# Feed-forward parts of a two-block network on one core: most chunks with the weights as stationary operand, without transposes

## The reference

```
def _rmsnorm(x, g):
    xf = x.astype(jnp.float32)
    y = xf * lax.rsqrt(jnp.mean(xf * xf, axis=-1, keepdims=True) + EPS)
    return (y * g.astype(jnp.float32)).astype(x.dtype)

def _swiglu(x, wg, wu, wd):
    return (jax.nn.silu(x @ wg) * (x @ wu)) @ wd

h = _swiglu(_rmsnorm(x, g[0]), ffn_w_gate[l, 0], ffn_w_up[l, 0], ffn_w_down[l, 0])
x = x + 0.5 * _rmsnorm(h, g[1])
```

## Time and profile before

| | |
|---|---|
| median of 3 runs | 1312.46 us (1311.19 to 1315.73) |
| span of the profiled execution | 1310.4 us, first to last instruction |
| its own time | not given apart from the span |
| TensorE busy, matmuls | 1287.3 us, 98% |
| VectorE busy | 783.8 us, 60% |
| ScalarE busy | 680.9 us, 52% |
| GpSimd busy | 118.8 us, 9% |
| granted TensorE clock, mean | 0.997 |
| memory traffic | 253.64 MB, mean 194 GB/s |

### The profile page before, as it was taken

The page is one execution under the profiler, slowest core; times in us unless marked ns, Lnnn a source line. Parts: engine busy times, 40 slices in busy tenths (PEclk is TensorE's granted clock), DMA queues, the critical chain, the costliest instruction groups (busy, mean ns, idle before and its releaser), DMA issues.

```text
span 1310.4 us, 18569 instructions
## 1 busy us (share of the span) xinstructions
PE 1287.3 (98%) x6815; PEld 1059.7 (81%) x6815; DVE 783.8 (60%) x1029; ACT 680.9 (52%) x1025; POOL 118.8 (9%) x120
## 2 busy tenths in 40 slices
PE   8999999999999999999999999999999999999997
PEld 7887788887788887877888888888887897888886
DVE  4477655454855556576655556655556677755554
ACT  4433643344744455557644447544556656745543
...
GB/s 336 380 402 211 140 295 203 180 187 177 161 193 192 192 203 182 194 178 91 195 194 180 183 200 146 207 192 192 185 231 98 185 152 102 189 191 183 181 206 54
DMA packets 177379, 253.64 MB, mean 194 GB/s; under 512 B 9352, under 2 KB 143796, under 8 KB 177332
## 3 DMA queue, kind: packets, MB, share of 16 engines
...
## 4 chain that ended last, share of the span: by engine, by line
PE 91%; DVE 4%; ACT 2%; SPq 1%; DMA 1%; issue 1%; DVEq 0%; ACTq 0%
PE ps L601 27%; PE ps L603 26%; PE ps L602 26%; PE ps L641 2%; PE ps L686 2%; PE ps L642 2%; PE ps L649 2%; PE ps L1011 1%; PE ps L625 1%; PE ps L883 1%; DMA raw<-in_conv_w_in 1%; SPq L480 1%; ACT L1177 1%; PE ps L872 1%; DVE x_sb L1714 1%
## 5 line engine op out<-in xcount | busy, mean ns | idle before, releaser
L1658 DVE TENSOR_TENSOR w_lo<-raw,w_hi 128x2048 fp32r<-128x2048 f32 x111 | 261.8, 2359 | 158.9 <-ACT w_hi L1189 158.8
L601 PE MATMUL ps<-w_lo,xT_hi 128*128 128x512 f32 x836 | 331.2, 396 | 1.0 <-DVE act_pair L1815 1.0
L603 PE MATMUL ps<-w_hi,xT_lo 128*128 128x512 f32 x836 | 326.2, 390 | 0.0
L602 PE MATMUL ps<-w_hi,xT_hi 128*128 128x512 f32 x836 | 325.7, 390 | 0.0
L1663 DVE SCALAR_TENSOR_TENSOR w_lo<-raw,par,w_hi 128x512 fp32r<-128x512 f32 x336 | 231.6, 751 | 133.2 <-ACT w_hi L1194 133.1
L1189 ACT ACTIVATE w_hi<-raw 128x2048 fp32r<-128x2048 f32 x111 | 212.2, 1913 | 152.3 <-PE ps L603 144.1
L1194 ACT ACTIVATE w_hi<-raw,par 128x512 fp32r<-128x512 f32 x336 | 214.4, 712 | 0.8 <-PE ps L603 0.8
L603 PEld LDWEIGHTS ps<-w_hi,xT_lo 128*128 128x128 f32 x836 | 156.9, 188 | 33.5
L601 PEld LDWEIGHTS ps<-w_lo,xT_hi 128*128 128x128 f32 x836 | 157.0, 188 | 33.3 <-DVE act_pair L1815 1.4
L602 PEld LDWEIGHTS ps<-w_hi,xT_hi 128*128 128x128 f32 x836 | 157.2, 188 | 31.4 <-issue 0.2
L601 PE MATMUL ps<-w_lo,hT_hi 128*128 128x512 f32 x400 | 156.5, 391 | 0.0
(11 more groups left out here) (256 smaller groups left out, 1497.1 us busy)
## 6 DMA issues: line engine op xcount, KB each, us to landing
...
```

The source lines that it names most:

```text
L601: pe.matmul(o, a_hi, b_lo, start=first, stop=False, skip_group_check=True)
L602: pe.matmul(o, a_hi, b_hi, start=False, stop=False, skip_group_check=True)
L603: return pe.matmul(o, a_lo, b_hi, start=False, stop=last, skip_group_check=True)
L1658: dve.tensor_tensor(w_lo[:, slot_of(n), :], raw[:, slot_of(n), :], w_hi[:, slot_of(n), :].bitcast(F32), ALU.subtract).then_inc(raw_done, 1)
```

## The change

In chunks 1 to 10 of every feed-forward part the first product is done the other way round. `wide_part` takes 128 columns of weights as stationary operand and all 256 tokens as moving one. For each of four column blocks (two of gates to banks 2 and 3, two of up to banks 0 and 1) and each input tile there are two matmuls: the low weights against `xT_hi`, 256 columns, and the high weights against `xT_hi` and `xT_lo` together, 512 columns, into the two halves of a bank. For the latter the two tensors become one, `xT_pair`. The sums come out with hidden columns on the partitions, which is what `down_part` needs, so these chunks have no transposes. Chunk 0 stays as it was, except that its turned form goes through bank 4.

The two halves of a bank have to be added. ScalarE copies the second half (`gate_rest`, `up_rest`) and VectorE adds the first. Tokens now lie along the columns, so r is needed as a row on every partition: `turn_r` makes it once a part with two transposes, ScalarE copies it to `r_cols`, and VectorE multiplies the gates by it. The up half isn't multiplied by r any more; as the result is normalised behind the part, the epsilon of that norm is scaled instead (`EPS_Y`).

TensorE's order in a chunk j is `next_wide(j)` (first unit), `wide_up(j)` (second unit), and `down(j)` for chunk j - 1. At the end of a part, `down` of chunk 9 is done for the first token tile and half of the second before the wait for the last chunk, and one group of six matmuls instead of twelve stays behind `y_tok0`. The table load on ScalarE stands between the last silu and the last up copy. In FFN0 the gate rows are summed between the groups of `down`, and ScalarE copies both behind `yT_hi`.

```diff
+        xT_pair = sb("xT_pair", [P, 2, KT, SEQ], F32R)
+        xT_hi, xT_lo = xT_pair[:, 0, :, :], xT_pair[:, 1, :, :]
         yT_hi = sb("yT_hi", [P, KT, SEQ], F32R)
         yT_lo = sb("yT_lo", [P, KT, SEQ], F32R)
...
-            def turn_hid(s, j):
+            def turn_hid(bank):
                 for f in range(2):
                     for t in range(TOKT):
-                        tr = pe.transpose(ps[:, 2, f * SEQ + t * P:f * SEQ + (t + 1) * P], hid[:, t, tok(f)], ident[:, :])
+                        tr = pe.transpose(ps[:, bank, f * SEQ + t * P:f * SEQ + (t + 1) * P], hid[:, t, tok(f)], ident[:, :])
                 tr.then_inc(hT_ps, 1)
+            def turn_r(s):
+                pe.wait_ge(x_rstd, 2 * x_event(s) + 2)
+                for t in range(TOKT):
+                    c = 2 * x_event(s) + t
+                    tr = pe.transpose(ps[:, 5, tok(t)], stat[:, 2, c:c + 1].to_broadcast([P, P]), ident[:, :])
+                tr.then_inc(r_ps, 1)
+            def wide_part(n, u, blocks, j=0):
+                hi, lo = unit(n, j)
+                for b in blocks:
+                    for k in range(4 * u, 4 * u + 4):
+                        c = slice((k % 4) * 512 + b * P, (k % 4) * 512 + (b + 1) * P)
+                        bank = WIDE_BANK[b]
+                        pe.matmul(ps[:, bank, 0:SEQ], lo[:, c], xT_hi[:, k, :], start=k == 0, stop=False, skip_group_check=True)
+                        mm = pe.matmul(ps[:, bank, :].rearrange("p (s c) -> p s c", s=2), hi[:, c], xT_pair[:, :, k, :],
+                                       start=False, stop=k == KT - 1, skip_group_check=True)
+                return mm
...
-                def chunk(n_a, j_hid, j, first):
-                    pe.wait_ge(hid_done, 2 * NCH * f + 1 + 2 * j_hid)
-                    up_part(n_a, 0, 0, j)
-                    pe.wait_ge(hid_done, 2 * NCH * f + 2 + 2 * j_hid)
-                    up_part(n_a, 0, 1, j).then_inc(w_used, 1)
-                    turn_hid(s, j_hid)
-                    up_part(n_a + 1, 4, 0, j).then_inc(up_tok0, 1)
-                    up_part(n_a + 1, 4, 1, j).then_inc(w_used, 1)
-                    pe.wait_ge(hT_ok, NCH * f + j_hid + 1)
-                    down_part(n_a + 2, hT_hi, hT_lo, 0, 0, first, False, j)
-                    down_part(n_a + 2, hT_hi, hT_lo, 0, 1, first, False, j).then_inc(w_used, 1)
-                chunk(n + 2, 0, 0, True)
-                with pe.Fori(1, NCH - 2) as i:
-                    chunk(n + 2, i, i, False)
+                v = WIDE * f
+                def wide_up(j):
+                    wide_part(n, 1, (0, 1), j).then_inc(gate_ps, 1)
+                    wide_part(n, 1, (2, 3), j).then_inc(w_used, 1)
+                def down(j):
+                    pe.wait_ge(hT_ok, NCH * f + j)
+                    down_part(n + 1, hT_hi, hT_lo, 0, 0, isinstance(j, int), False, j)
+                    down_part(n + 1, hT_hi, hT_lo, 0, 1, isinstance(j, int), False, j).then_inc(w_used, 1)
+                def next_wide(j):
+                    pe.wait_ge(gate_sum, v - 1 + j)
+                    wide_part(n - 1, 0, (0, 1), j)
+                    pe.wait_ge(up_sum, v - 1 + j)
+                    wide_part(n - 1, 0, (2, 3), j).then_inc(w_used, 1)
+                wide_part(n - 1, 0, (0, 1), 1)
+                pe.wait_ge(hid_done, 2 * f + 2)
+                wide_part(n - 1, 0, (2, 3), 1).then_inc(w_used, 1)
+                turn_hid(4)
+                if s in FOLDED:
+                    turn_r(s)
+                wide_up(1)
+                down(1)
+                with pe.Fori(2, NCH - 1) as i:
+                    next_wide(i)
+                    wide_up(i)
+                    down(i)
                 last = n + FFN_UNITS - 1
+                next_wide(NCH - 1)
+                wide_up(NCH - 1)
+                pe.wait_ge(hT_ok, NCH * (f + 1) - 1)
+                down_part(last - 1, hT_hi, hT_lo, 0, 0, False, False)
                 if s == FFN0:
+                    pe.wait_ge(gate_sum, v + WIDE)
                     pe.wait_ge(ada_p_done, ADA_CH)
                     gate_row(0)
-                pe.wait_ge(hid_done, 2 * (NCH * f + NCH - 1) - 1)
-                up_part(last - 3, 0, 0)
-                pe.wait_ge(hid_done, 2 * (NCH * f + NCH - 1))
-                up_part(last - 3, 0, 1).then_inc(w_used, 1)
-                turn_hid(s, NCH - 2)
-                up_part(last - 2, 4, 0).then_inc(up_tok0, 1)
-                up_part(last - 2, 4, 1).then_inc(w_used, 1)
+                down_part(last - 1, hT_hi, hT_lo, 0, 1, False, False, ks=(0,))
                 if s == FFN0:
                     pe.wait_ge(ada_row_a, 3)
                     gate_row(1)
-                pe.wait_ge(hT_ok, NCH * (f + 1) - 1)
-                down_part(last - 1, hT_hi, hT_lo, 0, 0, False, False, ks=(0,))
-                pe.wait_ge(hid_done, 2 * NCH * (f + 1))
-                turn_hid(s, NCH - 1)
-                down_part(last - 1, hT_hi, hT_lo, 0, 0, False, False, ks=(1,))
                 pe.wait_ge(hT_ok, NCH * (f + 1))
                 down_part(last, yT_hi, yT_lo, 0, 0, False, True).then_inc(y_tok0, 1)
-                down_part(last - 1, hT_hi, hT_lo, 0, 1, False, False).then_inc(w_used, 1)
+                down_part(last - 1, hT_hi, hT_lo, 0, 1, False, False, ks=(1,)).then_inc(w_used, 1)
                 down_part(last, yT_hi, yT_lo, 0, 1, False, True, ks=(0,))
                 if s + 1 in FOLDED:
                     turn_x(s + 1, 0)
...
-                def turned(j, dst):
-                    act.wait_ge(hT_ps, NCH * f + 1 + j)
-                    act.activation(dst, ps[:, 2, :].rearrange("p (f c) -> p f c", f=2), ACT.Copy).then_inc(hT_hi_ok, 1)
-                def chunk(j):
-                    if not (isinstance(j, int) and j == 0):
-                        split(n + 2, j)
-                    gates(j)
+                def turned(dst):
+                    act.wait_ge(hT_ps, f + 1)
+                    act.activation(dst, ps[:, 4, :].rearrange("p (f c) -> p f c", f=2), ACT.Copy).then_inc(hT_hi_ok, 1)
+                def wide_gate(j):
+                    act.wait_ge(gate_ps, WIDE * f + j)
+                    act.activation(gate_rest, ps[:, 2:4, SEQ:2 * SEQ], ACT.Copy).then_inc(gate_rest_ok, 1)
+                    if s in FOLDED:
+                        act.wait_ge(gate_ok, WIDE * (f - 1) + j)
+                    else:
+                        act.wait_ge(gate_sum, WIDE * f + j)
+                    act.activation(sil, gate_s, ACT.Silu).then_inc(sil_wide, 1)
+                def wide_up(j):
+                    act.wait_ge(w_used, v + 3 * j)
+                    act.activation(up_rest, ps[:, 0:2, SEQ:2 * SEQ], ACT.Copy).then_inc(up_rest_ok, 1)
+                def wide(j):
+                    split(n + 2, j)
+                    wide_gate(j)
+                    wide_up(j)
                     split(n + 3, j)
+                    act.wait_ge(hid_wide, WIDE * f + j)
+                    act.wait_ge(w_used, v + 1 + 3 * j)
+                    act.activation(hT_hi[:, :, :], hid, ACT.Copy).then_inc(hT_hi_ok, 1)
                     split(n + 4, j)
-                    turned(j, hT_hi[:, :, :])
                 if s in FOLDED:
                     act.wait_ge(x_rstd, 2 * x_event(s) + 2)
                 if s == FFN0:
                     act.wait_ge(gain_ok, 1)
-                chunk(0)
+                gates()
+                split(n + 3)
+                split(n + 4)
+                if s in FOLDED:
+                    act.wait_ge(r_ps, f)
+                    act.activation(r_cols, ps[:, 5, 0:SEQ], ACT.Copy).then_inc(r_ok, 1)
+                turned(hT_hi[:, :, :])
                 with act.Fori(1, NCH - 1) as j:
-                    chunk(j)
+                    wide(j)
                 def gate_row(h):
                     act.wait_ge(ada_ps, 4 + h)
                     act.activation(rows[:, 2, h * 512:(h + 1) * 512], ps[:, 3, :], ACT.Copy).then_inc(ada_row_a, 1)
+                split(n + FFN_UNITS - 1)
+                wide_gate(NCH - 1)
+                warm_up(ACT.Sqrt)
+                wide_up(NCH - 1)
+                act.wait_ge(hid_wide, WIDE * f + WIDE)
+                act.activation(yT_hi[:, 0:2, :], hid, ACT.Copy).then_inc(hT_hi_ok, 1)
                 if s == FFN0:
                     gate_row(0)
-                split(n + FFN_UNITS - 1)
-                gates(NCH - 1)
-                if s == FFN0:
                     gate_row(1)
-                warm_up(ACT.Sqrt)
-                turned(NCH - 1, yT_hi[:, 0:2, :])
                 split(n + FFN_UNITS)
...
-                def turned(j, dst, hi):
+                        dve.wait_ge(sil_done, 2 * f + t + 1)
+                        dve.tensor_tensor(hid[:, t, :], ps[:, t, FCH:2 * FCH], sil[:, t, :], ALU.mult).then_inc(hid_done, 1)
+                def turned(dst, hi):
+                    dve.wait_ge(hT_hi_ok, NCH * f + 1)
```

(49 more changed lines are left out.)

44 lines of the change are left out of this document (27 added, 17 removed).

## The result

The changed kernel takes 1323.13 us (median of 4 runs, 1320.28 to 1324.73) against 1312.51 (1311.19 to 1315.73): ratio 1.0075, 95% interval 1.006 to 1.009. It is slower, and the forecast of 1306.6 with its range to 1314 missed it. The profiled execution has a span of 1322.9 us at a mean granted clock of 0.991, 12.5 more than before where 5.9 less was forecast: 18.4 us to explain.

A forecast was written before the change was run, and what follows sets the result against it. TensorE's instruction stream, busy 98% of the span, was taken as the bound. Terms 10.4 - 22.3 + 0.7 - 0.8 + 6.1 = -5.9 us on span 1310.4, plus 2.1 around it, gave 1306.6 us, range 1298 to 1314.

The forecast's parts named there:

- 45 periods: Steady chunks, nine periods in each of five parts: the chunk period falls from 16.81 to 16.52 us.
- Part 1, the pair: Hidden half in wide form, 50 chunks: 32 pairs at 0.3464 us replace 48 matmuls of 512 columns, +10.4 us.
- a pair beyond 0.350: Wide pairs: a 256- plus 512-column pair taking over 0.350 us would make the prediction wrong; it assumed 0.3464.
- dearer pairs: Rival, chance 0.12: fetching x's second 256-column run costs another 13 ns a pair, +21 us, so 1328; decides from 3.7 ns.
- Part 2, transposes: Hidden chunk's transposes go except in each part's first chunk: 45 x 0.495 = -22.3 us.
- Part 3, starts: Part starts: `turn_r`'s added transposes cost +0.7 us; the first wide chunk not waiting for `hid_done` gives -0.8 us.
- Steady chunks, ScalarE and VectorE: Loop: added vector work costs nothing, with 3 us or more to spare everywhere under TensorE's 16.5 us.
- rival of late engines: Rival, chance 0.10: vector engines late in the loop; 0.12 us a chunk eats the gain, 0.5 gives 1331.
- Part 4, the last stretch: Ends of the five parts: later `y_tok0` and `turn_x`, 1.5 x 3 + 1.4 + 0.2 = +6.1 us.
- The clock falls: Rival, chance 0.20: waits of about 2.2 us ahead of AB and FOX lower TensorE's clock, 1.7 us each: 1310.0.
- Columns alone count: Rival, chance 0.08: 16 extra instructions a chunk cost nothing, 1296.2; with the skill's 2.5 ns a matmul, 1298.2.

The follow-up runs named there:

- pure streams: Changed kernel with the low products of the wide form left out, x fetched in two runs or in one: 1143.75 and 1142.19 us, one run each.
- four spacings of changes: Changed kernel, groups of four, groups of eight and mirrored kernel: 32, 8, 4 and 2 short-to-long changes a chunk, periods 16.792, 16.684, 16.613 and 16.573 us.
- mirrored kernel: Groups of eight with high products before low ones for the first two blocks, low before high for the other two: 1308.03 us, ratio 0.9968.
- groups of eight: Changed kernel with old unit order, table load behind the next part's first split, x side by side, eight low then eight high products: 1310.26 us, ratio 0.9978.
- order alone: Kernel before, with only six `down` matmuls of the second token tile moved ahead of the wait for the last chunk: 1316.67 us, ratio 1.003.
- groups of four: Changed kernel with four low products, then four high ones, for each column block: 1316.11 us, ratio 1.0027.
- groups of four (both): Groups of four, and the same with old order of last units and table load behind the next part's first split: 1316.11 and 1313.41 us.
- late table with old order: Changed kernel with the table load behind `yT_hi` and the six moved `down` matmuls back behind `y_tok0`: 1320.18 us, ratio 1.0053.
- x in one run: Changed kernel with both halves of x side by side for each input tile, so 512 moving columns are contiguous: 1321.26 us, ratio 1.0062.
- other bank: Changed kernel with low products of one block alternating with high ones of the other, never the same bank twice running: 1321.61 us, ratio 1.0072.
- three of 256: Changed kernel with each 512-column matmul of the wide pair cut into two of 256 columns: 1330.11 us, ratio 1.0127.
- late table: Changed kernel with ScalarE's table load for the root moved behind `yT_hi`: 1322.9 us, ratio 1.0069.

## Why the prediction was wrong, step by step

| term | forecast | in the profiled executions |
|---|---|---|
| 45 periods | -12.9 | -0.6 |
| starts of FFN1 to FFN4, to the first `down` | +0.7 | +2.8 |
| last stretches | +6.1 | +6.5 |
| opening, to FFN0's first `down` | +0.2 | +3.8 |

The forecasts sum to -5.9, the findings to +12.5. The pairs of chunk 1, 0.2 in each part, stand ahead of the first `down`. The 45 periods are 45 x (16.792 - 16.805). For FFN0's last stretch I count against its 2.9 us the 1.35 by which its loop lost a gate row with the restart.

- **Part 1, the pair: the step that failed.** "I take the sum of the two rows, as both neighbours pay the same 13 ns". Both rows are from streams of one size. Back to back, 256 then 512 columns cost 0.3531 and not 0.3464, and `down` pays another 0.05 a chunk behind the last pair. 45 x (32 x 6.7 ns + 0.05) is 11.9 of the 12.3 us by which the 45 periods miss, and these are two thirds of the whole miss. The prediction's own sign of being wrong, a pair beyond 0.350, came true. The rival "dearer pairs" had the direction right; its size was 13 ns a pair, twice what was found, though it saw that 3.7 would decide. Its mechanism was wrong: the fetch in two runs costs nothing, in the mixed stream and in the pure one. Shown by the pure streams and by the four spacings of changes.
- **The evidence was in the earlier trace rows.** From 906.27 to 911.85 are 24 steps behind the transposes: 5.58 us, where 24 x 0.2266 are 5.44. The first step alone has 0.09 of these 0.14, by this line of the same timeline:

```profile
906.59 0.40 PE L602 MATMUL ps<-w_hi,xT_hi 128*128 128x512 f32 x1
```

  The other 0.05 lie in the steps behind it, as many as `down` pays behind the pairs: the long matmuls behind short ones were slow there too. The prediction booked these 0.14 us as part of the transposes' price, which was right for the removal, and did not ask whether matmuls of 256 columns would do the same.
- **Part 2, transposes:** right. The groups of hidden transposes are 20 and not 220, and with the dear changes spread out their saving shows: the mirrored kernel's period is 0.23 us below that of before.
- **Part 3, starts:** 0.7 forecast, 2.8 found: 0.2 in FFN1, 1.0 in FFN2, 0.4 in FFN3 and 1.2 in FFN4. FFN2 and FFN4 hold the two falls of the clock (below). In FFN1 the wait for `hid_done` went as forecast, but its 0.8 us weren't won. The changed kernel has its third fall there, and groups of eight, without that fall, wait 0.66 us for `w_lo` and 0.32 for `xT_pair`; both need about 28.2 us from `turn_x` to the first `down`, and the kernel before needed 28.0. The forecast's 0.7, the 0.8 not won, two falls at 0.6 and the dearer pairs (4 starts x 32 x 6.7 ns = 0.9) would make 3.6, 0.8 more than was found; that wasn't taken apart.
- **Steady chunks, ScalarE and VectorE:** right. No wait in the loop, busy times within 0.2 us. The rival of late engines is out.
- **Part 4, the last stretch:** right to 0.4 us in sum, and in FFN2 to 0.1 us at both marks. The order alone in the kernel before cost 3.9 us in the time. What I missed is that the order and the table load could be had otherwise.
- **"The clock falls", 0.20:** came true beside the failed step, at both places. From AB's first transpose to FFN2's first `down` the changed kernel needs 648.22 - 530.04 = 118.18 us. The kernel in groups of eight, with a wait of 0.87 there and the clock full (timeline and window of that kernel):

```profile
522.72 0.44 PE L644 MATMUL ps<-ident,xn 128*128 128x128 f32 x2 [0.87 <-DVE xn L1823]
...
640.12 0.39 PE L620 MATMUL ps<-w_lo,hT_hi 128*128 128x512 f32 x1
```

```profile
523.00:527.00 4.00, 3.66 (x20) 2.67 (x18) 3.96 (x6) 3.16 (x7) 0.00 (x0) 1.00 0.00 0
```

  needs 117.40, 0.8 us less, and at FOX it is 148.36 against 147.55. One wide chunk lies in each of these stretches, 0.18 dearer in the changed kernel by the table above, so about 0.6 is the clock's. In the kernel before with the new order, whose matmuls are those of before, the fall at FOX cost 148.39 - 147.20 = 1.2. The rival had 1.7 each, taken from a stretch full of matmuls; here the stage has waits of its own, which may hide a part (not taken apart). By the Trainium skill ("TensorE: Matmul & The Clock Gate", Part 1: The HAM clock gate) the engine slows down after idleness; the trace agrees here. But a wait as long doesn't always bring the fall. The groups of four wait 2.23 us at AB as well (first transpose at 523.35), TensorE is as idle ahead of it, and the clock stays. Windows of that kernel ahead of this start and behind it:

```profile
519.35:523.35 4.00, 1.77 (x15) 1.50 (x14) 3.96 (x8) 2.74 (x6) 0.00 (x0) 1.00 0.29 111
523.35:527.35 4.00, 3.66 (x19) 2.81 (x20) 3.93 (x7) 2.87 (x6) 0.00 (x0) 1.00 0.00 0
```

  The kernels profiled, those without low products left out, have 14 waits of 2.2 to 2.4 us ahead of AB and FOX, and 11 of them were followed by a fall; of the 10 waits of 0.87 to 1.05 us none was.
- **"Columns alone count", 0.08:** out. The 2.5 ns a matmul of the Trainium skill (same page, Wait — 56ns, not 53.3ns?) are not what the pure stream of 32 shows, which is 13 ns beyond its columns.
- **The opening:** no edit lies there but for the first chunk's pairs and the banks, so nearly all of these 3.8 us are chance, and they go with the granted clock. The same window in the changed kernel and, below, in the kernel before:

```profile
28.00:36.00 8.00, 7.83 (x40) 7.83 (x41) 4.23 (x9) 2.16 (x4) 1.45 (x2) 0.57 1.09 361
28.00:36.00 8.00, 8.00 (x66) 7.03 (x67) 3.91 (x9) 1.84 (x3) 1.45 (x2) 1.00 1.09 361
```

  8 x (1 - 0.57) = 3.4 us of full clock are missing. Just ahead of it TensorE waited 1.60 us for ScalarE, and 0.67 in the kernel before. The clocks of two windows and the first `down` of FFN0, over all kernels profiled but those without low products:

| clock 28 to 36 | clock 144 to 152 | kernels | first `down` |
|---|---|---|---|
| 1.00 | 1.00 | groups of four (both), late table with old order, mirrored | 165.0 to 165.3 |
| 1.00 | 0.79 | before, x in one run | 166.3, 166.7 |
| 0.79 | 1.00 | other bank, order alone, groups of eight | 166.5 to 167.1 |
| 0.79 | 0.79 | three of 256, late table | 168.8, 168.3 |
| 0.57 | 0.79 | changed kernel | 170.1 |

  So 3.8 us of the profiled difference hang on when the clock fell in two single executions; the difference of the medians is 10.6 and not 12.5.

**What stays open:** what in TensorE makes the five long matmuls behind a short one slow. The runs show when it is paid and how much, and that neither the bank, nor the fetch of x, nor which operand is stationary matters. Whether other pairs of sizes pay the same wasn't tried, except that the earlier trace rows show it behind 128 columns. It is open, too, why three of the 14 long waits left the clock at full.
